# The value projection of a spatial gating layer: seven products of quarters in place of eight, with operand sums on GpSimd

## The reference, cut to what matters

```python
z = h @ w_in                         # h: 512x1024 (normed), w_in: 1024x6144
u, v, g = jnp.split(z, 3, axis=-1)   # each 512x2048
v = layer_norm(v, ln_g, ln_b)
sv = jnp.einsum('gts,bcsgd->bctgd', wsm, v) + bs.T[:, :, None]
y = u * sv * jax.nn.silu(g)
return y @ w_out
```

## Time and profile before

| | us |
|---|---|
| median of the runs | 1315.51 |
| span of the profiled execution | 1314.1 |
| TensorE busy | 1295.6 (99%) |
| VectorE busy | 758.1 (58%) |
| ScalarE busy | 642.3 (49%) |
| GpSimd busy | 343.7 (26%) |

### The profile page before, as it was taken

One profiled execution on the slowest core, in us unless ns is written; L12 is line 12 of the kernel. 1 busy time (PEld: TensorE's weight loads), 2 busy tenths in 40 slices (PEclk: granted clock), 3 DMA queues, 4 the chain that ended last, 5 costly groups with the idle time before them and its releaser, 6 DMA issues.

```text
span 1314.1 us, 17855 instructions
## 1 busy us (share of the span) xinstructions
PE 1295.6 (99%) x6478; PEld 1086.5 (83%) x6478; DVE 758.1 (58%) x1209; ACT 642.3 (49%) x1164; POOL 343.7 (26%) x393
## 2 busy tenths in 40 slices
PE   7999999999999999999999999999999999999998
PEld 6998778788888888888888888889888888888986
DVE  5656889735652226898444653335467335578843
ACT  5379888624432325998244433414234234355632
POOL 2238877400000007773000000000000000668620
PEclk9999999999999999999999999999999999999999
DMA  5332100132232232001323333332332421421121
GB/s 192 84 108 65 45 25 15 53 106 97 81 99 97 99 99 73 17 0 32 112 97 93 87 93 97 96 97 64 87 110 82 135 96 49 129 65 49 33 64 65
DMA packets 70867, 104.66 MB, mean 80 GB/s; under 512 B 3476, under 2 KB 31368, under 8 KB 70664
## 3 DMA queue, kind: packets, MB, share of 16 engines
q1 hardware_dynamic: 69584, 99.44, 24.3%
q0 software_dynamic: 1088, 4.17, 1.1%
q10 hardware_dynamic: 120, 0.05, 0.0%
HBM read 101.55 MB, written 2.10 MB: 79 GB/s over the span
## 4 chain that ended last, share of the span: by engine, by line
PE 89%; DVE 5%; issue 3%; ACT 2%; DMA 1%; SPq 0%; DVEq 0%; POOL 0%; ACTq 0%; POOLq 0%
PE ps L496 24%; PE ps L498 23%; PE ps L497 23%; PE ps L700 3%; PE ps L1006 2%; PE ps L858 2%; PE ps L713 1%; PE ps L950 1%; PE ps L679 1%; PE ps L727 1%; PE ps L848 1%; DVE sp L2086 1%; PE ps L849 1%; PE ps L728 1%; DVE sp_l L2091 1%
## 5 line engine op out<-in xcount | busy, mean ns | idle before, releaser
L1689 DVE TENSOR_TENSOR w_lo<-stage,w_hi 128x1024 fp32r<-128x1024 f32 (+4 forms) x188 | 224.1, 1192 | 415.1 <-ACT w_hi L1108 414.9
L1108 ACT ACTIVATE w_hi<-stage 128x1024 fp32r<-128x1024 f32 (+4 forms) x188 | 191.0, 1016 | 457.2 <-PE ps L498 456.8
L496 PE MATMUL ps<-a0h,w_hi 128*128 128x512 f32 x512 | 204.5, 399 | 1.1 <-DVE q_lo L2273 0.8
L498 PE MATMUL ps<-a0h,w_lo 128*128 128x512 f32 x512 | 199.9, 390 | 0.0
L497 PE MATMUL ps<-a0l,w_hi 128*128 128x512 f32 x512 | 199.5, 390 | 0.0
L2375 POOL TENSOR_TENSOR small<-small 128x16 f32<-128x16 f32 (+2 forms) x14 | 32.3, 2311 | 388.0 <-DVE small L1767 284.4
L496 PE MATMUL ps<-w_hi,a0h 128*128 128x512 f32 (+1 forms) x320 | 121.9, 381 | 0.1
L498 PE MATMUL ps<-w_hi,a0l 128*128 128x512 f32 (+1 forms) x320 | 119.9, 375 | 0.0
L497 PE MATMUL ps<-w_lo,a0h 128*128 128x512 f32 (+1 forms) x320 | 119.8, 374 | 0.0
L496 PEld LDWEIGHTS ps<-a0h,w_hi 128*128 128x128 f32 x512 | 96.2, 188 | 20.5 <-DVE w_lo L1689 1.3
L498 PEld LDWEIGHTS ps<-a0h,w_lo 128*128 128x128 f32 x512 | 96.1, 188 | 20.6
(11 more groups left out here) (330 smaller groups left out, 2840.0 us busy)
## 6 DMA issues: line engine op xcount, KB each, us to landing
stage<-in_a_w_in SPq DMA_DIRECT2D x48, 512.0 KB, 3.7
stage<-in_ple_w_gate SPq DMA_DIRECT2D x16, 512.0 KB, 3.3
stage<-in_w_kv_shared SPq DMA_DIRECT2D x16, 512.0 KB, 3.6
stage<-in_sb_w_in SPq DMA_DIRECT2D x16, 512.0 KB, 3.7
stage<-in_a_w_out SPq DMA_DIRECT2D x16, 512.0 KB, 3.4
stage<-in_b_w_in SPq DMA_DIRECT2D x16, 512.0 KB, 3.7
stage<-in_mla_w_in SPq DMA_DIRECT2D x8, 512.0 KB, 3.9
stage<-in_sb_w_out SPq DMA_DIRECT2D x8, 512.0 KB, 3.4
```

Source lines behind the costliest of these rows:

```text
L496: pe.matmul(bank, wh, mh, start=start and not seeded, stop=False, skip_group_check=seeded)
L498: return pe.matmul(bank, wl, mh, start=False, stop=stop, skip_group_check=seeded)
L1108: act.activation(slab(w_hi[r % 2], L, nk, w), slab(stage[r % 4], L, nk, w), ACT.Copy).then_inc(S("hi_ready"), 1)
L1689: dve.tensor_tensor(slab(w_lo[r % 2], L, nk, w), slab(stage[r % 4], L, nk, w), slab(w_hi[r % 2], L, nk, w), ALU.subtract)\
```

## The change

`g_v` is computed as two halves u of 1024 columns. In each half the activations (512 tokens x 1024) and the weights (1024 x 1024) are cut into four quarters, and the eight products of quarters become seven (Strassen's scheme in Winograd's form). A product is named by its weight operand: quarters B11, B12, B21, B22 as loaded (B12 only enters sums), and sums T1 = B12-B11, T2 = T1-B22, T3 = B12-B22, T4 = T2+B21 (in signs as the kernel has them). Each operand is two pieces s of 256 rows; a piece now serves two tiles of 128 tokens, so 12 matmuls. The orders are

```diff
# tensor engine
+                if L.name == "gate1" and g == 1 and k >= 4:
+                    if k == 6:
+                        for n in range(4):
+                            for j in range(4, KD):
+                                mm = products(j, n)
+                                if n == 3 and j == 5:
+                                    mm.then_inc(S("ring_used"), 1)
+                            mm.then_inc(S("ring_used" if n == 3 else "gate1_bank"), 1)
+                    continue
...
+        def g_v_product(u, name, banks, k0, first):
+            for s in range(2):
+                r = operand(u, name, s)
+                pe.wait_ge(S("lo_ready"), r + 1)
+                for m in range(2):
+                    for k in (2 * s, 2 * s + 1):
...
+        g_v_product(0, "B11", 0, 0, True)
+        pe.wait_ge(S("s_lo"), 1)
+        g_v_product(0, "T3", 2, None, True)
+        pe.wait_ge(S("g_read"), 8)
+        token_sums(2, ps[7], 0)
+        pe.wait_ge(S("v_act"), 2)
+        g_v_product(0, "B21", 0, 4, False)
...
# scalar engine
+            if r in (V0, V0 + 1):
+                act.wait_ge(S("ring_used"), r - 2)
+            elif r >= 2 and r != V0 - 1:
                 act.wait_ge(S("ring_used"), r - 1 + turn * 8)
...
+        def last_gate(read):
+            L = lin["gate1"]
+            for j in range(4):
+                split_to(L.load0 + j + 1)
+            for j in range(4):
+                split_to(L.load0 + 4 + j + 1)
+                if j < 2:
+                    group_done(L, 0)
+                    for n in (2 * j, 2 * j + 1):
+                        read(L, 0, n, ps[4 * (L.group0 % 2) + n])
+            for n in range(4):
+                if n == 3:
+                    sum_hi("T3", 1, s3_raw[:, :, :])
+                    split_to(V0 + 1)
+                    group_done(L, 1)
+                else:
+                    act.wait_ge(S("gate1_bank"), n + 1)
+                read(L, 1, n, ps[4 * ((L.group0 + 1) % 2) + n])
...
+        split_to(operand(0, "T3", 1))
+        act.wait_ge(S("ring_used"), operand(0, "B11", 1) + 1)
+        act.wait_ge(S("s_lo"), 1)
+        for m in range(2):
+            act.activation(v_tile(0, 0, m), bank_of(m), ACT.Copy).then_inc(S("v_act"), 1)
+        sum_hi("T1", 2, h_raw[:, 4:KD, T // 2:T])
+        split_to(operand(0, "B21", 1))
+        sum_hi("T2", 3, h_raw[:, 0:4, 0:T // 2])
+        split_to(operand(0, "T1", 0))
...
# vector engine (last_gate, from the second group's splits on)
+            dve.wait_ge(S("ring_used"), V0 - 2)
+            for k in range(4):
+                h_rows(k)
+            for n in range(4):
+                if n == 3:
+                    sum_lo("T3", 1, s3_raw[:, :, :])
+                    split_to(V0 + 1)
+                read(L, 1, n, ps[4 * ((L.group0 + 1) % 2) + n])
+            dve.wait_ge(S("ring_used"), V0)
+            for k in range(4, KD):
+                h_rows(k)
...
+        split_to(operand(0, "B22", 1))
+        dve.wait_ge(S("ring_used"), operand(0, "T2", 1) + 1)
+        for m in range(2):
+            v_add(0, 1, m, 2 + m, 1, 2, 8)
+        for m in range(2):
+            v_add(0, 1, m + 2, 2 + m, 1, 4, 8)
+        split_to(operand(0, "T4", 1))
...
-        linear("g_u", normed_to(ug, 2), [v_moments, v_shift], near=True)
+        linear("g_u", normed_to(ug, 2), [v_stats(g) for g in range(4)] + [v_moments, v_shift, ws_lows, nothing, nothing, nothing, nothing, ws_bias], near=True)
...
# sync engine: a quarter is two transfers of 512 KB
+        def g_v_loads():
+            sp_.wait_ge(S("o2_read"), HEADS)
+            quarter(0, "B11")
+            quarter(0, "B12")
+            sp_.wait_ge(S("act_lo"), first_item["p1"] + 2)
+            quarter(0, "B21")
+            sp_.wait_ge(S("lo_ready"), V0)
+            quarter(0, "B22")
...
# gpsimd
+        for s in range(2):
+            weights_in(0, "B12")
+            weights_in(0, "B22")
+            pool.wait_ge(S("lo_ready"), V0 - 3 + s)
+            weight_sum(0, "T3", s)
+        for s in range(2):
+            weights_in(0, "B11")
+            weight_sum(0, "T1", s)
+        low, high = slice(0, T // 2), slice(T // 2, T)
+        pool.wait_ge(S("h_raw"), 4)
+        pool.tensor_tensor(s3_raw[:, :, :], h_raw[:, 0:4, high], h_raw[:, 0:4, low], ALU.subtract).then_inc(S("s_raw"), 1)
+        pool.wait_ge(S("h_raw"), KD)
+        pool.tensor_tensor(h_raw[:, 4:KD, high], h_raw[:, 0:4, high], h_raw[:, 4:KD, high], ALU.add).then_inc(S("s_raw"), 1)
+        for s in range(2):
+            pool.wait_ge(S("lo_ready"), operand(0, "B11", s) + 1)
+            weight_sum(0, "T2", s)
...
```

More of the change, by code:

```diff
@@ L571, in group, with linear @@
                     mm.then_inc(S("ring_used"), 1)
-        def linear(name, r=None, before={}, late={}, second={}):
+        def linear(name, r=None, before={}, late={}, second={}, third={}):
             L = lin[name]
@@ L925, in ws_sums @@
         def ws_sums():
-            G = lin["g_v"].group0
+            G = lin["g_u"].group0 + 1
             pe.wait_ge(S("ws_ok"), 4)
@@ L941, in _ @@
+        g_v_product(1, "T2", 4, None, True)
+        pe.wait_ge(S("v_dve"), 14)
+        g_v_product(1, "B22", 0, None, False)
+        pe.wait_ge(S("v_dve"), 16)
+        g_v_product(1, "T3", 4, None, False)
+        pe.wait_ge(S("v_act"), 16)
+        g_v_product(1, "B21", 6, 4, False)
+        pe.wait_ge(S("v_dve"), 20)
+        g_v_product(1, "T4", 4, 4, False)
+        linear("g_u", third={6: ws_sums})
         assert lin["g_g"].group0 % 2 == 0
@@ new lines, in _ @@
+        v_add(0, 1, 1, 3, -1, 0, 8)
+        sum_lo("B22", 4, h_raw[:, 4:KD, 0:T // 2])
+        split_to(operand(0, "T2", 1))
+        dve.wait_ge(S("rstd_done"), 3)
+        dve.tensor_copy(rstd[:, :], ps[7][:, :]).then_inc(S("rstd_ok"), 1)
+        dve.wait_ge(S("ring_used"), operand(0, "T1", 1) + 1)
+        for m in range(2):
+            v_add(0, 1, m + 2, 4 + m, 1, 0, 8)
+        split_to(operand(0, "B22", 1))
+        dve.wait_ge(S("ring_used"), operand(0, "T2", 1) + 1)
+        for m in range(2):
+            v_add(0, 1, m, 2 + m, 1, 2, 8)
@@ new lines, in _ @@
+        for m in range(2):
+            v_add(0, 1, m + 2, 2 + m, 1, 4, 8)
+        split_to(operand(0, "T4", 1))
+        dve.wait_ge(S("ring_used"), operand(0, "B22", 1) + 1)
+        for m in range(2):
+            v_add(0, 1, m, 4 + m, 1, 6, 8)
+        split_to(operand(1, "B11", 1))
+        dve.wait_ge(S("ring_used"), operand(0, "T4", 1) + 1)
+        for m in range(2):
+            v_add(0, 0, m + 2, 2 + m, 1, 0, 8)
+        split_to(operand(1, "T2", 1))
+        dve.wait_ge(S("ring_used"), operand(1, "T1", 1) + 1)
@@ new lines, in _ @@
+        for m in range(2):
+            v_add(1, 1, m + 2, m, 1, 0, 16)
+        split_to(operand(1, "B22", 1))
+        dve.wait_ge(S("ring_used"), operand(1, "T2", 1) + 1)
+        for m in range(2):
+            v_add(1, 1, m, 4 + m, 1, 0, 16)
+        split_to(operand(1, "T3", 1))
+        dve.wait_ge(S("ring_used"), operand(1, "B22", 1) + 1)
+        for m in range(2):
+            v_add(1, 1, m, m, 1, 16, 16)
+        split_to(operand(1, "B21", 1))
+        dve.wait_ge(S("ring_used"), operand(1, "T3", 1) + 1)
@@ L2165, in v_moments @@
+        for m in range(2):
+            v_add(1, 1, m + 2, 4 + m, 1, 14, 16)
+        split_to(V_END)
+        dve.wait_ge(S("ring_used"), operand(1, "T4", 1) + 1)
+        for m in range(2):
+            v_add(1, 0, m + 2, 4 + m, 1, 0, 16)
         def v_moments():
@@ new lines, in _ @@
+        pool.wait_ge(S("s_raw"), 3)
+        pool.tensor_tensor(h_raw[:, 4:KD, low], h_raw[:, 4:KD, low], h_raw[:, 0:4, low], ALU.add).then_inc(S("s_raw"), 1)
+        for s in range(2):
+            pool.wait_ge(S("lo_ready"), operand(0, "T3", s) + 1)
+            weights_in(0, "B21")
+            weight_sum(0, "T4", s)
+        for s in range(2):
+            weights_in(1, "B11")
+            weights_in(1, "B12")
+            pool.wait_ge(S("lo_ready"), operand(0, "B22", s) + 1)
+            weight_sum(1, "T1", s)
@@ L2534, in _ @@
+        for s in range(2):
+            weights_in(1, "B22")
+            pool.wait_ge(S("lo_ready"), operand(0, "T4", s) + 1)
+            weight_sum(1, "T2", s)
+        for s in range(2):
+            weight_sum(1, "T3", s)
+        for s in range(2):
+            weights_in(1, "B21")
+            pool.wait_ge(S("lo_ready"), operand(1, "B11", s) + 1)
+            weight_sum(1, "T4", s)
         root(bn_rs, MB, "bn_in", 1, "bn_ok")
```

311 lines of the change are left out of this document (256 added, 55 removed).

## The result

Before 1315.5 us, after 1345.3 us (1344.0 to 1346.3): 1.0225 times as long, 95% interval 1.0211 to 1.0240. The profiled execution has a span of 1343.5 us where the prediction had 1342.4. First the page, and the windows of gate1's second group, g_v and g_u; they answer to the earlier trace rows.

A forecast was written before the change was run, and what follows sets the result against it. TensorE bounds the kernel, busy 1295.6 of 1314.1 us. The terms -10.9 + 3.7 + 13.8 + 3.9 + 9.8 + 8.0 = +28.3 us gave a span of 1342.4 and a median of 1343.8 us, range 1322 to 1357.

The forecast's parts named there:

- sums that take turns with VectorE: GpSimd and VectorE instructions reading two SBUF tensors alternate, VectorE first at a boundary; forecast 1334 to 1350 us, chance 0.60.
- Matmuls: g_v goes from 384 to 336 matmuls, 48 fewer at 0.2267 us each: -10.9 us.
- gate1's end: In gate1's second group TensorE waits for the split of the last weight piece, queued behind the first group's reads: +3.7 us.
- B11's second half: In g_v, its split waits behind T3's activation sum, needing s3_raw after four GpSimd weight sums: +13.8 us, bounds 5.7 and 16.
- T3's first half: Before it TensorE waits because VectorE does 6.6 us of other work after B11's split: +3.9 us.
- rival 2: TensorE starts slowly after waits, matmuls 0.43 us apart, 1.9 us each after four or so waits: 1351 us, chance 0.15.
- Other activation sums: In g_v, waits at B21 2.0, T1's halves 5.2 and 1.0, T2's first 1.6: +9.8 us, without turns 1.8.
- Rest of g_v: Ten remaining GpSimd weight sums each hold up a split by 0 to 2.5 us: +8.0 us, bounds 3.3 and 15.
- Slow starts: Matmul starts 0.43 us apart behind TensorE's waits; not in the forecast sum, listed as a sign of being wrong.
- At nothing: Counted as costing no time: statistics and mixing-weight work under g_u, and v_add, which reads one PSUM tensor.
- Rival 1: No turns: VectorE and GpSimd run side by side, B11's wait is 9.0 us; +10.8 us, 1326, chance 0.17.
- Rival 3: Faster: GpSimd sums of 1.3 us or less, so B11's second half hardly waits; 1314 at 1.0 us, chance 0.05.

The follow-up runs named there:

- experiment 3: Kernel after the change, with each GpSimd sum made by four instructions of 128x256, same values: 1345.1 us, ratio 1.0231.
- experiments 10: Seven products in the second half only, layer norm ahead of scaled rows and activation sums, three slots for that half's pieces: 1320.8 us, 1.0041 times the kernel before.
- 12: The second-half kernel of experiments 10 with all weight and activation sums on VectorE, behind splits of the first half: 1309.4 us, 0.9952 times the kernel before.
- 4: Kernel after the change, with all GpSimd sums but s3_raw covering only 16 columns, the rest left unsummed: 1323.0 us, ratio 1.0054.
- experiment 1: Kernel after the change, with gate1's last piece split one step earlier on ScalarE and VectorE, ahead of the first group's reads: 1342.9 us, ratio 1.0203.
- Experiment 8: Kernel after the change, with three slots for g_v's pieces, VectorE splitting one piece further ahead from T2 on, one GpSimd-issued transfer behind g_v: 1337.0 us, 1.0167.
- experiment 5: Kernel after the change, with matmuls that nothing reads filling four long TensorE waits: 1342.1 us, ratio 1.0202.
- experiment 6: Kernel after the change, with the sixteen weight sums moved from GpSimd to VectorE, activation sums staying on GpSimd: 1333.6 us, ratio 1.0136.

## Why the prediction was right, step by step

The time was met within 1.5 us. The cause that it named, sums that take turns with VectorE, is shown by the rows of the kernel after beside those of experiment 3, by VectorE's rows of experiments 10 and 12, and by the times of 4 and 12. The terms were less good than their sum, and that the sum came so close is in part luck:

- **Matmuls**, -10.9: 48 fewer, as counted.
- **gate1's end**, +3.7: a wait of 3.76 us, as argued, and experiment 1 removes it. The 1.6 us of slow start behind it were not in the sum.
- **B11's second half**, +13.8: 10.69. B22 landed at 726.9 (726.5 expected), the sums take 2.4 us alone, and the chain of releases is the one described. Off is how turns fall: at a boundary one VectorE instruction goes first, not all seven that are queued, so `s3_raw` was done at 740.5, not 743.8. VectorE's leftovers then came behind it and took 1.9 us of that back, which leaves 1.5. The other 1.6 us of the difference are TensorE's, which came there that much later after its slow start. (The upper bound of 16 us for this wait does not come out of the prediction's own figures: five sums of 3.4 to 3.7 us give 13.9 to 15.4.)
- **T3's first half**, +3.9: 1.59. VectorE's part was exact, 752.59 - 745.93 = 6.66 us against 6.6, `h_rows` of 0.41 us included. TensorE came 2.3 us later, since B11's second half started slowly; that slow start only took from this wait, as rival 2 said of it.
- **Other activation sums**, +9.8: 3.57 for B21, 1.05 and 3.32 for T1's halves, none before T2: 7.9. The whole is near, the shares are not: 2.0, 5.2, 1.0 and 1.6 were given. T1's second half waited for something that had been left out: the five `TENSOR_SCALAR` of the norm stand ahead of its split on VectorE and took 5.4 us, 3.06 of it for four that took 0.88 before.
- **Rest of g_v**, +8.0: 7.1 us, in eight waits behind which the next matmul starts 0.5 to 1.9 us later than usual. Experiment 8 shows that they hang on the ring's margin: 8.4 us go with a third slot, while the sums stay on GpSimd. Whether each begins with a split held up by a sum, as the prediction followed them, was not traced.
- **Slow starts**, 0 in the sum: 35 matmuls at 0.43 us, 7.6 us, of which experiment 5 gets 3.2 back. The prediction named matmuls 0.43 us apart behind the waits as a sign of being wrong, and it came: rival 2's mechanism took place beside the turns, with 0.15 of the chances. Its 1351 did not, since 1.6 us behind gate1 and 2.3 behind B11 only shortened the next wait; 3.7 are left, and should have stood in the sum.
- **At nothing**: the statistics and mixing weights under g_u, right (89.0 us, no wait); `v_add`, right (1.40 us for two, whatever GpSimd did).

Together: 3.76 + 10.69 + 1.59 + 7.9 + 7.1 + 7.6 - 10.9 = +27.7, of the 29.4 us between the two spans; the rest was not assigned. The largest single error is the slow starts, 7.6 us at nothing. Of these, 3.9 came off B11's and T3's waits and so leave the sum as it was. Against the other 3.7 stand waits that were put too high: 1.5 in B11's by the rule that VectorE goes first with all that it has queued, 1.9 in the other activation sums, 0.9 in the rest of g_v, 4.3 together. That these cancel is luck.

Rival 1 is out by experiment 3 and by the five lengthened instructions above. Rival 3's condition did not occur: a sum takes 2.4 us, not 1.3.

The Trainium skill, "SBUF — State Buffer", section "Who interferes with whom", has more that bears on this than the prediction used: it names `tensor_scalar` among the operations that can take the shared ports with one tensor. The trace agrees (the norm's four took 3.06 us in place of 0.88). The prediction counted by number of inputs alone, and so had the norm's instructions at nothing.

## What to carry to other kernels

Before work moves to an idle engine, ask what it shares with the engine that feeds the bound: here a GpSimd sum kept a VectorE instruction off for up to 2.2 us (2.89 in place of 0.68), and VectorE does the same sum in 1.2. Where matmuls are saved in a stage, compare the other engines' work with the shorter stage, and halve the saving if that is what fits: seven products in one half, with all sums on VectorE and time to prepare them, took 1309.4 us, seven in both halves 1327.3 at best, there with the activation sums still on GpSimd. A piece that is halved may need a deeper ring, since its margin shrinks by more than half (2.8 to 0.1 us by the prediction's rows); a third slot gave 8.4 us.

## What the runs showed of the hardware that was not expected

- **Turns are not always one for one.** From 727 to 740 VectorE and GpSimd alternate, an instruction each. At 750.13 a GpSimd sum that came from idling took 5.72 us, while VectorE's low part, square sum and both splits (749.97 to 753.6) ran through, each in its usual time: by the rows the sum waited for all four. Both cases are in the rows above; what decides between them was not tested.
- **A short `TENSOR_SCALAR` takes its turn too.** A 128x4 one (L2451) took 2.37 us; in experiment 6, away from GpSimd's sums, it took 0.16. The 128x512 ones of `h_rows` take 0.41 us alone, where a `TENSOR_TENSOR` of that size takes 0.69; the Trainium skill, "VectorE: DVE Perf Modes", section "Mode 2×_2P — use both read ports for one tensor", says that an operation with one SBUF tensor can read it over both read ports, two results a cycle, and that `tensor_tensor` can't. The 0.41 and 0.69 us agree with that, and a second port in use would explain the turn; no run here tests it.
- **TensorE's clock fell while it stood idle, and useless work held it up.** In the last 8.9 us of idling up to 745.93 the granted clock was 0.68 on average (the last but two of the figures in the row below); behind waits of 3.3 us and more the first 7 to 11 matmuls ran 0.43 us apart, the 1.2 GHz level, behind waits of 1.59 and 1.05 us none did. The length of the wait alone does not decide it: in experiment 3 the first seven ran slowly behind a wait of 2.27 us, in experiment 8 none behind one of 3.02. With products that nothing reads in the waits they ran 0.23 us apart, and the kernel was 3.2 us shorter. The Trainium skill, "TensorE: Matmul & The Clock Gate", section "What's actually happening", states that an idle array is throttled; experiment 5 agrees.

```profile
737.00:745.93 8.93, 0.00 (x1) 0.01 (x1) 8.89 (x9) 3.62 (x5) 3.46 (x2) 0.68 0.00 0
```
